# The first half of the third gated layer in seven block products for 18 of its 22 pairs of tiles, with weight sums made in DRAM, and the modulation rows computed in two layers instead of three

## The reference

```python
def _modulated_norm(h, gain, shift, scale):
    return _rms_norm(h, gain) * (1.0 + scale) + shift

def _swiglu(h, w1, w2):                      # w1: 1024 x 5632, w2: 2816 x 1024
    a, b = jnp.split(h @ w1, 2, axis=-1)
    return (jax.nn.silu(a) * b) @ w2

mx = (cond_x @ ada_w[i] + ada_b[i])          # for the latent tokens
mc = (cond_c @ ada_w[i] + ada_b[i])          # for the context tokens: 9 x 1024 shifts, scales and gates a block layer
x = x + 0.5 * mx_gate * _swiglu(_modulated_norm(x, norm_g[i, 0], ...), ffn_w1[i, 0], ffn_w2[i, 0])
ctx = ctx + 0.5 * mc_gate * _swiglu(_modulated_norm(ctx, norm_g[i, 0], ...), ffn_w1[i, 0], ffn_w2[i, 0])
```

## Time and profile before

| | |
|---|---|
| time, median of 3 runs | 2773.91 us (2767.69 to 2777.02) |
| the profiled execution: time | 2775.72 us |
| the profiled execution: span | 2773.9 us |
| granted TensorE clock, mean over the span | 0.987 of full speed |
| PE busy | 98% of the span |
| POOL, DVE, ACT busy | 53%, 52%, 43% |
| DMA | 384.11 MB, mean 138 GB/s |

### The profile page before, as it was taken

The page is one execution under the profiler, slowest core; times in us unless marked ns, Lnnn a source line. Parts: engine busy times, 40 slices in busy tenths (PEclk is TensorE's granted clock), DMA queues, the critical chain, the costliest instruction groups (busy, mean ns, idle before and its releaser), DMA issues.

```text
span 2773.9 us, 52909 instructions
## 1 busy us (share of the span) xinstructions
PE 2709.3 (98%) x21984; PEld 2390.5 (86%) x21984; DVE 1454.0 (52%) x2776; ACT 1187.2 (43%) x2123; POOL 1476.2 (53%) x809
## 2 busy tenths in 40 slices
PE   8999999999999999999999999999999999999999
PEld 6888888778888888889888896899998799898999
DVE  4777406656663676505766124453175676613560
ACT  5222225435554322224222245644445666555553
POOL 4444443444334444444444442388886377595887
PEclk9999999999999999999999999999999999999999
DMA  8665432210001455424555326265564253353465
GB/s 308 211 210 196 139 99 84 94 61 4 4 27 61 169 193 169 152 92 146 187 176 173 110 93 137 69 197 185 168 190 151 70 164 118 115 177 128 155 195 160
DMA packets 106549, 384.11 MB, mean 138 GB/s; under 512 B 11431, under 2 KB 16712, under 8 KB 104776
## 3 DMA queue, kind: packets, MB, share of 16 engines
q1 hardware_dynamic: 87880, 313.61, 35.2%
q10 hardware_dynamic: 18432, 67.12, 6.9%
HBM read 375.44 MB, written 5.24 MB: 137 GB/s over the span
## 4 chain that ended last, share of the span: by engine, by line
PE 90%; ACT 3%; DVE 2%; POOL 2%; DMA 1%; issue 1%; SPq 0%; ACTq 0%
PE bank L236 25%; PE bank L238 24%; PE bank L237 24%; PE bank L1088 2%; POOL weights_lo L229 1%; PE upper_banks L236 1%; PE upper_banks L238 1%; PE upper_banks L237 1%; PE upper_banks L1890 1%; PE upper_banks L1873 1%; PE bank L1864 1%; PE upper_banks L1065 1%; PE bank L1202 1%; PE upper_banks L1135 1%; PE upper_banks L1213 1%
## 5 line engine op out<-in xcount | busy, mean ns | idle before, releaser
L229 POOL TENSOR_TENSOR weights_lo<-weights_landing,weights_hi 128x1024 fp32r<-128x1024 f32 x554 | 1341.9, 2427 | 1147.5 <-ACT weights_hi L219 1141.0
L219 ACT ACTIVATE weights_hi<-weights_landing 128x1024 fp32r<-128x1024 f32 x554 | 587.2, 1060 | 1140.7 <-PE bank L238 1032.0
L236 PE MATMUL bank<-normed_hi,weights_lo 128*128 128x256 f32 (+1 forms) x2776 | 922.2, 332 | 6.1 <-ACT normed_hi L707 1.9
L238 PE MATMUL bank<-normed_hi,weights_hi 128*128 128x256 f32 (+1 forms) x2776 | 914.9, 330 | 0.0
L237 PE MATMUL bank<-normed_lo,weights_hi 128*128 128x256 f32 (+1 forms) x2776 | 911.7, 328 | 0.0
L236 PEld LDWEIGHTS bank<-normed_hi,weights_lo 128*128 128x128 f32 x2776 | 522.3, 188 | 66.1 <-issue 4.4
L237 PEld LDWEIGHTS bank<-normed_lo,weights_hi 128*128 128x128 f32 x2776 | 522.4, 188 | 51.6
L238 PEld LDWEIGHTS bank<-normed_hi,weights_hi 128*128 128x128 f32 x2776 | 522.3, 188 | 51.4
L236 PE MATMUL bank<-hidden_hi,weights_lo 128*128 128x256 f32 (+1 forms) x1026 | 339.1, 331 | 0.0
L238 PE MATMUL bank<-hidden_hi,weights_hi 128*128 128x256 f32 (+1 forms) x1026 | 338.6, 330 | 0.0
L237 PE MATMUL bank<-hidden_lo,weights_hi 128*128 128x256 f32 (+1 forms) x1026 | 337.3, 329 | 0.0
(11 more groups left out here) (469 smaller groups left out, 3691.9 us busy)
## 6 DMA issues: line engine op xcount, KB each, us to landing
weights_landing<-w_up SPq DMA_DIRECT2D x176, 512.0 KB, 3.5
ada_rows<-w_ada_rows ACTq DMA_DIRECT2D x128, 512.0 KB, 4.3
weights_landing<-w_down SPq DMA_DIRECT2D x88, 512.0 KB, 3.5
weights_landing<-w_dn SPq DMA_DIRECT2D x33, 512.0 KB, 3.5
weights_landing<-w_mlp_up SPq DMA_DIRECT2D x32, 512.0 KB, 3.5
weights_landing<-w_mlp_down SPq DMA_DIRECT2D x32, 512.0 KB, 3.5
weights_landing<-w_gate SPq DMA_DIRECT2D x24, 512.0 KB, 4.2
weights_landing<-w_xbc SPq DMA_DIRECT2D x24, 512.0 KB, 3.5
```

The source lines that it names most:

```text
L219: k.nc.scalar.activation(k.WH[:, u % SLOTS, :], k.W[:, u % LANDS, :], ACT.Copy).then_inc(*k.AC.mark(("unit hi", u)))
L229: k.nc.gpsimd.tensor_tensor(k.WL[:, u % SLOTS, :], k.W[:, u % LANDS, :], k.WH[:, u % SLOTS, :].bitcast(F32), ALU.subtract).then_inc(*k.PO. ...
L236: nc.tensor.matmul(out, ll, rh, start=start, stop=False, skip_group_check=True)
L238: return nc.tensor.matmul(out, lh, rh, start=False, stop=stop, skip_group_check=True)
```

## The change

Three things change together.

**Seven products.** For pairs 4 to 21 of mlp10 the product is seen as a product of 2 x 2 blocks: tokens (context, latent) by depth (tiles 0 to 3, tiles 4 to 7) by columns (a, b). Eight block products become seven, by Winograd's form of Strassen's scheme. Two pairs make a group; nine groups. A block product is 4 depths x 3 matmuls x 256 columns for each of the group's two pairs, with one weight unit. Blocks p1, p2 and p4 use plain quarters of the weights, p3, p5, p6 and p7 use four sums of quarters. The token side has four mixes (three new operands, and one that takes the place of the upper latent half). DVE combines the results from the banks with subtractions of 256 columns.

**Sums in DRAM.** The four weight sums (9 units each) are made in DRAM while the first two gated layers run. SP copies a quarter from DRAM to a DRAM buffer, 36 copies of 512 KB: 18 in the first layer's first half, 18 in its second half. POOL then issues 36 accumulating DMAs on those: 18 in the first layer's second half, 9 in the second layer's first half, 9 in its second half.

**Rows.** mlp10 computes no rows any more; mlp00 takes 64 and mlp01 64, where it was 48, 40 and 40.

```diff
-ROWS = {"mlp00": (16, 64), "mlp01": (64, 104), "mlp10": (104, 144)}
+ROWS = {"mlp00": (16, 80), "mlp01": (80, 144)}
```

The blocks and their order; False is a plain quarter, True a sum:

```diff
+GROUPED, PLAIN = 9, 4
+BLOCKS = {"p1": (False, 0), "p2": (False, 1), "p4": (False, 3), "p5": (True, 0), "p6": (True, 1), "p7": (True, 2), "p3": (True, 3)}
+WINO = [(b, g - 1 if b == "p4" else g) for g in range(GROUPED) for b in ("p1", "p4", "p6", "p2", "p7", "p5", "p3") if b != "p4" or g]
+WINO.append(("p4", GROUPED - 1))
+SUM_OF = {0: (2, 3), 2: (0, 2), 1: (0, None), 3: (1, None)}
```

In the norm ahead of mlp10 ACT keeps a float32 copy beside `normed_hi`:

```diff
         act.wait_ge(*k.DV.after(norm, "scaled", d, c))
+        if norm == "norm10":
+            k.nc.scalar.activation(k.x32[:, d, half_tokens(c)], scaled_at(k, d), ACT.Identity,
+                                   bias=parts[c][3](d)).then_inc(*k.AC.mark((norm, "x32", d, c)))
```

The mixes: DVE makes them before its first pair, ACT rounds them behind the first silu, POOL subtracts:

```diff
+def mixes_act(k, act):
+    for m in range(3):
+        act.wait_ge(*k.DV.after("mix", m))
+        k.nc.scalar.activation(k.t_hi[:, m], k.t32[m][:], ACT.Copy).then_inc(*k.AC.mark(("mix", "hi", m)))
+def wino_pool(k, pool):
...
+    feed_pool(k, pool, F.base["w_up10"] + 5)
+    for m in range(3):
+        low(m, k.t_lo[:, m])
+    feed_pool(k, pool, F.base["w_wino"] + SLOTS)
+    low(3, k.n_lo[:, 0:4, CTX:TOK])
+    feed_pool(k, pool, F.base["w_down10"] + SLOTS)
```

The products on PE (waits cut), and the accumulating transfers on POOL:

```diff
+def wino_pe(k, pe):
...
+            for d in range(4):
+                at = (4 * j + d) * P
+                w = k.WH[:, u % SLOTS, at:at + P], k.WL[:, u % SLOTS, at:at + P]
+                mm = three(k.nc, bank_of(k, into[b], j), w, wino_operand(k, b, d), b in first and d == 0, d == 3)
...
+def add_pool(k, pool, stream, sums, every):
...
+    for n, (m, g) in enumerate(todo):
+        feed_pool(k, pool, at + n)
+        add_one(k, pool, m, g)
+def add_one(k, pool, m, g):
+    of = k.sums[m // 2, g] if SUM_OF[m][1] is None else k.dram["w_quarters"][SUM_OF[m][1], g]
+    pool.dma_start(k.sums[m, g], of, accum_op=ALU.add, max_dma_last_dim=8192).then_inc(k.sum_added[m], 16)
```

On SP the copies stand before loads of the same streams, without a wait; all four sums are waited for before the first unit of w_wino:

```diff
+        if u in begin:
+            m, g = begin[u]
+            sp.dma_start(k.sums[m, g], dram["w_quarters"][SUM_OF[m][0], g]).then_inc(k.sum_begun[m], 16)
+        if u == F.base["w_wino"]:
+            for m in range(4):
+                sp.wait_ge(k.sum_added[m], 16 * GROUPED)
```

More of the change, by code:

```diff
@@ L786, in up_act @@
     nc = k.nc
-    for n in range(2 * FT):
+    for n in range(up_tiles(st)):
         p = n // 2
@@ L799, in up_act @@
             rows_dma(k, act, st, p)
+        if n == 0 and st == "mlp10":
+            mixes_act(k, act)
 def up_dve(k, dve, st, tokens, hi, lo):
     nc = k.nc
-    for p in range(FT):
+    for p in range(up_tiles(st) // 2):
         s = k.sil[:, p % 2, 0:tokens]
@@ new lines, in wino_pe @@
+def wino_pe(k, pe):
+    F = k.F
+    into = {"p1": "X", "p2": "X", "p6": "Y", "p5": "Y", "p7": "Z", "p4": "Z", "p3": "V"}
+    first = ("p1", "p6", "p7", "p3")
+    mixed = {"p5": 0, "p6": 1, "p7": 2, "p4": 3}
+    for m, (b, g) in enumerate(WINO):
+        u = F.base["w_wino"] + m
+        pe.wait_ge(*k.PO.after("unit lo", u))
+        if b in mixed and g == 0:
+            pe.wait_ge(*k.PO.after("mix", "lo", mixed[b]))
+        for j in range(2):
+            if b == "p1" and g:
+                pe.wait_ge(*k.AC.after("wino", "silu ctx", g - 1, j))
+            if b == "p6" and g:
+                pe.wait_ge(*k.DV.after("wino", "raw lat", g - 1, j))
+            if b == "p7":
+                pe.wait_ge(*(k.DV.after("mlp10", "raw", PLAIN + 2 * g - 2 + j) if g else k.DV.after("mlp10", "raw", 2) if j else k.AC.after("mlp10", "silu", 2)))
+            if b == "p3":
+                pe.wait_ge(*(k.AC.after("wino", "silu lat", g - 1, j) if g else k.DV.after("mlp10", "raw", 3) if j else k.AC.after("mlp10", "silu", 3)))
+            if b == "p2":
+                pe.wait_ge(*k.AC.after("wino", "copy", g, j))
+            if b == "p5":
+                pe.wait_ge(*k.DV.after("wino", "u", g, j))
+            if b == "p4":
+                pe.wait_ge(*k.DV.after("wino", "b lat", g, j))
+            for d in range(4):
+                at = (4 * j + d) * P
+                w = k.WH[:, u % SLOTS, at:at + P], k.WL[:, u % SLOTS, at:at + P]
+                mm = three(k.nc, bank_of(k, into[b], j), w, wino_operand(k, b, d), b in first and d == 0, d == 3)
+            mm.then_inc(*k.PE.mark(("wino", b, g, j), *([("unit used", u)] if j else [])))
@@ new lines, in wino_act @@
+def wino_act(k, act):
+    nc, F = k.nc, k.F
+    hi = hidden(k, TOK)[0]
+    base = F.base["w_wino"]
+    nc.scalar.activation(k.n_hi[:, 0:4, CTX:TOK], k.t32[3][:], ACT.Copy).then_inc(*k.AC.mark(("mix", "hi", 3)))
+    for m, (b, g) in enumerate(WINO):
+        feed_act(k, act, min(base + m + SLOTS, len(F.source)))
+        for j in range(2):
+            if b == "p1" and g:
+                wino_lat_act(k, act, g - 1, j)
+            if b == "p1":
+                act.wait_ge(*k.PE.after("wino", "p1", g, j))
+                act.wait_ge(*(k.DV.after("wino", "a lat", g - 1, j) if g else k.PO.after("mix", "lo", 0)))
+                nc.scalar.activation(k.w_first[:, j, :], bank_of(k, "X", j), ACT.Copy).then_inc(*k.AC.mark(("wino", "copy", g, j)))
+            if b == "p6" and g:
+                wino_high_act(k, act, hi, g - 1, j)
+            if b == "p2":
+                act.wait_ge(*k.PE.after("wino", "p2", g, j))
+                act.wait_ge(*k.DV.after("mlp10", "lo", PLAIN + 2 * g + j - 2))
+                nc.scalar.activation(k.sil[:, j, 0:CTX], bank_of(k, "X", j), ACT.Silu).then_inc(*k.AC.mark(("wino", "silu ctx", g, j)))
+    for j in range(2):
+        wino_lat_act(k, act, GROUPED - 1, j)
+    for j in range(2):
+        wino_high_act(k, act, hi, GROUPED - 1, j)
```

151 lines of the change are left out of this document (142 added, 9 removed).

## The result

The changed kernel takes 2819.05 us (median of 4 runs, 2810.31 to 2829.75), the kernel before 2775.47 beside it; the ratio is 1.0168, 95% interval 1.0131 to 1.0205. It is 1.7% slower, and the time lies 15 us above the predicted range.

A forecast was written before the change was run, and what follows sets the result against it. PE, busy 98% of the span, was taken as the bound. Third layer -14.5 us and rows in two layers +23.3 sum to +8.8 on the profiled 2775.7, 2784.5; stated as 2783 for the median, range 2766 to 2804.

The forecast's parts named there:

- Sums in DRAM: Copies and accumulating transfers in the first two layers: POOL's five issues at down's start hidden, 0 us; other bound 21.
- Rival C: First layer's down: traffic or POOL's issues starve the weight units, more likely +10 to +25 us, 2795 to 2810; chance 0.15.
- Rows in two layers: First two layers: three rows a pair, loads issued in the pair itself, make DVE late and PE stall; +23.3 us.
- The stall before hidden_lo: Down's first tile, first and second layer: PE waits for the last hidden_lo, 4.5 and 9.1 us.
- The block products: Third layer's nine product groups: seven products for eight at PE's pace, 197.4 to 178.6 us, -18.8, plus 0.5 at the tail.
- rival D: Third layer: products do not run at PE's pace, 1 us wait per group costs 9 and more, 2787 to 2795; chance 0.13.
- The mixes: Third layer: three mixes_lo before weight unit 5 idle PE 3.0 us, plus 2.0 for the clock and 0.5 in the norm.
- Rows leave the third layer: Third layer: the 16 transposes there go, -1.7 us; DVE's 40 row computations bring nothing back.
- The 2.50 us of hidden_lo: First layer, DVE: hidden_lo takes 2.50 us because it waits for a POOL unit that began before it.
- Rival B: First two layers: a pair's first row is there when hidden_lo ends, nothing stalls; -14.5 us, 2760; chance 0.12.

The follow-up runs named there:

- rows ahead: The changed kernel with each row load issued one place earlier (four loads ahead instead of three): 2757.63 us, ratio 0.9950; run again, 2761.31 us, 0.9961.
- copies: The changed kernel with the 36 DRAM copies but without the accumulating transfers: 2790.58 us, ratio 1.0051 to the kernel before.
- no-sums: The changed kernel without copies or accumulating transfers, w_wino reading plain quarters of the weights: 2790.27 us, ratio 1.0059 to the kernel before.
- the mixes' edit: The changed kernel with row loads one place earlier and POOL's three mixes_lo behind weight unit 8 instead of 5: 2752.59 us, ratio 0.9933.

## Why the prediction was wrong

**The step that failed is "Sums in DRAM", the term taken at 0.** It asked what five issues cost POOL, and for these five it was right: 4.18 us, nowhere near the 16 of cover. (It did not look at the eighth, which holds POOL for 15.76 us in the kernel with rows ahead; that this stayed within the cover is luck.) It also said that nobody waits for a sum before w_wino, which holds. It did not ask who else uses the DMA engines while the transfers run, in the very stretch for which it had just computed that DVE would be 16 to 21 us late. They cost 29.9 us: 22.6 for the bursts at the start of the two down stages, 7.3 for the rest. Rival C came nearest (2795 to 2810, "traffic or POOL's issues starve the weight units") but held another mechanism: weight units starved of data in the first layer's second half. Weight loads did slow to 15 us and were covered; the rows starved, and the weight unit that PE missed was held by order, behind a square that waited for DVE.

By the marks of the profiled execution the kernel came out at +40.4 instead of +8.8: 29.9 for the transfers, 8.6 more for the rows, 3.9 less in the third layer and 3.1 less in the rest, where no matmul was changed.

**Rows in two layers** was right in mechanism and small in size: +23.3 predicted, +26.6 in the kernel that has this edit alone, 30.7 and 33.7 in copies and no-sums. Three rows took 11.8 to 12.3 us in most of its pairs, 11.92 + 0.15 predicted. Where the lag was paid was predicted less well. The stall before hidden_lo came out at 4.58 and 4.66 where 4.5 and 9.1 stood; that the first agrees is luck, since the lag was larger than forecast and part of it was paid before. The lag grew faster than forecast: the product of pair 15 began at 247.91, and ten pairs of 10.99 us after pair 5 of before are 232.8. That is a lag of 15.1 us, at the 15.8 that the banks bear; from there on each pair gave PE an idle of 0.6 to 0.8 us, and down had less left to wait for.

**What the forecast missed about lag** is that it changes what a later transfer costs. In the kernel with rows ahead the last row of the second layer, loaded beside that layer's burst, took 16.5 us to land instead of 4.3, DVE began it at 1165.82, and that down stage lost nothing (-0.4). With DVE late each such load is on the path. The same transfers cost about 30 us and nothing that can be measured.

**The block products** ran at PE's pace in every group, and rival D is out: in the changed kernel POOL is busy 147.83 of 166.10 us and PE in all. The stage gained 18.4 us in the changed kernel, against 14.5 predicted with the mixes in it. 4.4 of it is a faster pace of its matmuls (last section); at the pace of the earlier trace rows it gained 14.0. The two kernels with the mixes unchanged that kept that pace throughout gained 13.5 and 13.7; the one with copies, all at the faster pace, 21.1. **The mixes** cost 3.40 us of idle (3.0 predicted). **Rows leave the third layer** gave 1.1 in both kernels that have only this there, for 1.7. One remark beside the sum is wrong: 0.517 for 0.5 costs 3% of the time of the products, but of the gain it takes a quarter, from 197.4 / 8 = 24.7 us to 18.8. The sum itself has it right. The 2.50 us of hidden_lo that the prediction explains are pair 5's, its working is pair 6's (2.01).

Rival B (the saving stands) decided by whether the first row is there when hidden_lo ends. It was priced at 2760, and the one edit that makes its condition true gave 2757.63 and 2761.31. A late pair then takes 9.67 us and not the 10.99 of its working, which only makes its case stronger.

## What to carry to other kernels

Before a transfer is costed at nothing because no one waits for it, list the loads in flight beside it and the engine that waits for each, and ask whether that engine is on time: in an in-order program a late engine can turn a slower load into a stall. Look also at what stands behind the late work in its own program and who waits for that (here evictions, then squares, then weights). If an engine falls behind because all its loads are issued in the step that uses them, one load in flight ahead may be worth more than the work that the change saves (here 61 us against 18).

## What the runs showed of the hardware

**Accumulating transfers are slow on the DMA engines, and the first seven are cheap on POOL.** Between 318 and 352 us, 560 packets of q0 carried 3.67 MB in 53.1% of 16 engines' 34 us, 0.52 us each and 12.7 KB per us and engine. The row loads' q10 did 1.57 MB in 11.7%, 24.7 KB per us. So an accumulated byte costs twice a loaded one, and five issues cost POOL 4.18 us. The Trainium skill, DMA: Bandwidth & Descriptors, Anatomy of one DMA, fits 2.0 us plus the bytes over 436e3 per us, by which one is an estimated 3.2 us; the trace has 6.2 to 8.7 us for the nine single ones beside the second layer's first half, and a median of 18.2 for the seven that went beside pair 21's rows. The same page says (SWDGE vs HWDGE vs iDMA) that an engine takes its queues in turn. The rows fit that, without proving it: all three queues moved data in the stretch, and a row load took 18.0 us beside a queue that had seven transfers in it.

**Every ninth of POOL's transfers found an empty queue.** In all six profiles of kernels with the transfers the 8th, 17th, 26th and 35th began only when all earlier ones had landed. Where they had not, POOL stood, and the issue began 0.25 to 0.26 us after the last landing: at 333.21 after 332.96 with rows ahead (15.76 us of idle), at 332.93 and 1178.37 in its second execution (14.10 and 10.28). Other issues found up to five in flight and did not wait. What limits it these traces don't say.

**The clock after a short idle.** After the 10.95 us matmuls come at 355.56, 356.15, 356.58: 0.43 us apart, where they were 0.23. In the stretch 350 to 360 us the granted clock is 0.53, the lower level (1.2 GHz) in its busy part.

**The 256-column matmul has two paces at full clock.** The kernel with rows ahead ran twice under the profiler. Windows of the products, first execution, then the second:

```profile
1380.00:1400.00 20.00, 20.00 (x179) 20.00 (x178) 9.21 (x18) 11.79 (x17) 18.64 (x9) 1.00 0.64 206
...
1460.00:1480.00 20.00, 20.00 (x172) 20.00 (x171) 11.06 (x17) 10.70 (x17) 17.07 (x8) 1.00 0.60 188
```

```profile
1380.00:1400.00 20.00, 20.00 (x172) 20.00 (x171) 9.76 (x17) 10.27 (x16) 17.11 (x8) 1.00 0.59 186
```

PE is busy throughout, the granted clock is 1.00, and yet 20 us hold 179 matmuls or 172. I took the time from start to start in the products: it is 0.1133 us for 1151 of them and 0.1178 for 358 in the first execution, 0.1178 for all 1511 in the second (two single intervals of 0.23 in the first aside). In the changed kernel's profile it is 0.1133 for 984 and 0.1178 for 526, which is 984 x 0.0045 = 4.4 us in its favour. Over the 1512 matmuls of the products the two paces are 6.7 us apart. The third layer's gain of the same kernel was 20.1 and 13.5, and 1151 x 0.0045 = 5.2 of these 6.6 us are the pace of the products. Before, all 1009 intervals that I took in the fourth layer (from 1795 us on) are the slower one, and so the forecast took it; in the second execution of rows ahead 1023 of 1044 there are the faster, which is part of its -11.3 in the rest. I found nothing in these traces that says what sets it; it stays open. It also warns against reading a few us out of two single profiles: the mixes' edit shows no gain against the first execution of rows ahead (-18.8 against -20.1) and 5.3 us against the second.
